# Input projection and gated linear attention of a hybrid layer put into one program of slots, with half of the projection's weights reloaded

## The reference

```python
x = layer_norm(x, ln_in_g, ln_in_b)
gq, gk, gv, gr, glow, sq, sk, sv, cb, cc, ch = split_cols(x @ w_in)      # 1024 -> 3088 columns
lg = jax.nn.log_sigmoid((glow @ w_gate_up + b_gate).astype(f32)) / GLA_TAU
# gla_chunk, by chunks of 64 tokens:
b = jnp.cumsum(lg, axis=2)
att = jnp.einsum('bhtk,bhsk,bhtsk->bhts', q, k, decay)                   # decay = exp(b_t - b_s), s <= t
o = (jnp.einsum('bhtk,bhkv->bhtv', q * jnp.exp(b), S)
     + jnp.einsum('bhts,bhsv->bhtv', att, v))
S_new = (jnp.exp(b_last[:, :, 0, :])[..., None] * S
         + jnp.einsum('bhsk,bhsv->bhkv', k * jnp.exp(b_last - b), v))
# then
go = go * lax.rsqrt(jnp.mean(go * go, axis=-1, keepdims=True) + LN_EPS) * gla_norm_g * jax.nn.silu(gr)
cy, conv_state = short_conv(cc * ch, conv_prev, conv_w)                  # causal, 3 taps
co = cb * cy
```

## Time and profile before

| | |
|---|---|
| median of three runs (3108.27 to 3112.32) | 3112.1 us |
| the profiled execution, its own time | 3112.73 us |
| its span, first to last instruction | 3110.9 us |
| mean granted clock of TensorE | 0.934 of full speed |
| PE busy | 2734.4 us, 88% |
| DVE busy | 1505.1 us, 48% |
| ACT busy | 1069.5 us, 34% |
| POOL busy | 329.9 us, 11% |
| HBM traffic | 168 GB/s over the span |

### The profile page before, as it was taken

One profiled execution on the slowest core, in us unless ns is written; L12 is line 12 of the kernel. 1 busy time (PEld: TensorE's weight loads), 2 busy tenths in 40 slices (PEclk: granted clock), 3 DMA queues, 4 the chain that ended last, 5 costly groups with the idle time before them and its releaser, 6 DMA issues. The chain is left out here.

```text
span 3110.9 us, 38667 instructions
## 1 busy us (share of the span) xinstructions
PE 2734.4 (88%) x13838; PEld 2268.3 (73%) x13838; DVE 1505.1 (48%) x2247; ACT 1069.5 (34%) x1783; POOL 329.9 (11%) x283
## 2 busy tenths in 40 slices
PE   5999999946662467999998999999999988999997
PEld 4787789835541356888877888877888766888885
DVE  5333342158883556665656544446644425522224
ACT  3323333223342424443443444443434321322221
POOL 1100010056600000000001100001100000000000
PEclk9999999966786588999999999999999989999998
DMA  5544454233315654575655766565766554544452
GB/s 185 169 160 153 160 180 126 85 121 88 89 45 187 191 191 140 169 249 179 216 193 191 229 218 209 191 206 183 234 190 227 170 171 144 190 157 158 154 168 98
DMA packets 362107, 526.11 MB, mean 169 GB/s; under 512 B 28832, under 2 KB 208208, under 8 KB 361920
## 3 DMA queue, kind: packets, MB, share of 16 engines
q1 hardware_dynamic: 337696, 480.23, 48.1%
q10 hardware_dynamic: 18832, 26.10, 2.3%
q0 software_dynamic: 5392, 17.31, 1.6%
HBM read 422.74 MB, written 100.80 MB: 168 GB/s over the span
## 5 line engine op out<-in xcount | busy, mean ns | idle before, releaser
L111 PE MATMUL p_ps_u<-p_xh,p_wh 128*128 128x512 f32 (+1 forms) x1280 | 453.1, 354 | 5.4 <-DVE p_xl L1626 5.4
L112 PE MATMUL p_ps_u<-p_xh,p_wl 128*128 128x512 f32 (+1 forms) x1280 | 451.5, 353 | 0.0
L113 PE MATMUL p_ps_u<-p_xl,p_wh 128*128 128x512 f32 (+1 forms) x1280 | 451.0, 352 | 0.0
L1575 DVE SCALAR_TENSOR_TENSOR p_res<-p_res,p_ps_d 128x512 f32<-128x512 f32 (+1 forms) x340 | 232.1, 685 | 451.4 <-PE p_ps_d L113 445.7
L111 PE MATMUL p_ps_d<-p_wh,p_hh 128*128 128x512 f32 (+1 forms) x1088 | 433.2, 398 | 16.9 <-DVE p_res L1575 14.8
L112 PE MATMUL p_ps_d<-p_wh,p_hl 128*128 128x512 f32 (+1 forms) x1088 | 428.6, 394 | 0.0
L113 PE MATMUL p_ps_d<-p_wl,p_hh 128*128 128x512 f32 (+1 forms) x1088 | 428.4, 394 | 0.0
L1484 ACT ACTIVATE p_wh<-p_wst 128x1024 fp32r<-128x1024 f32 x288 | 293.9, 1049 | 276.6 <-PE p_ps_d L113 225.0
L1633 DVE TENSOR_TENSOR p_r<-p_r 128x512 f32<-128x512 f32 (+1 forms) x160 | 95.8, 599 | 461.3 <-ACT p_hh L1514 461.3
L1507 ACT ACTIVATE p_r<-p_ps_u 128x512 f32<-128x512 f32 (+1 forms) x160 | 83.8, 524 | 579.5 <-PE p_ps_u L113 579.4
L111 PEld LDWEIGHTS p_ps_u<-p_xh,p_wh 128*128 128x128 f32 x1280 | 241.2, 188 | 35.5 <-DVE p_xl L1626 6.2
(11 more groups left out here) (155 smaller groups left out, 4473.0 us busy)
## 6 DMA issues: line engine op xcount, KB each, us to landing
p_wl<-wlo_scratch SPq DMA_DIRECT2D x216, 512.0 KB, 5.1
p_wst<-in_w_up SPq DMA_DIRECT2D x128, 512.0 KB, 6.0
p_wst<-in_w_down SPq DMA_DIRECT2D x128, 512.0 KB, 4.6
wlo_scratch<-p_wl SPq DMA_DIRECT2D x72, 512.0 KB, 3.6
p_wst<-in_w_in SPq DMA_DIRECT2D x128, 256.0 KB, 3.6
p_kk<-ks_scratch SPq DMA_DIRECT2D x84, 256.0 KB, 5.9
p_vv<-vs_scratch SPq DMA_DIRECT2D x84, 256.0 KB, 4.5
p_wst<-in_w_out SPq DMA_DIRECT2D x32, 512.0 KB, 6.0
```

What stands on the lines that cost most here:

```text
L111: pe.matmul(out, lhs_hi, rhs_hi, start=first, stop=False, skip_group_check=skip)
L112: pe.matmul(out, lhs_lo, rhs_hi, start=False, stop=False, skip_group_check=skip)
L113: return pe.matmul(out, lhs_hi, rhs_lo, start=False, stop=last, skip_group_check=skip)
L1575: dve.scalar_tensor_tensor(out=acc, in0=acc, scalar=scale, in1=ps_d[:c, d % DB, :], op0=ALU.mult, op1=ALU.add).then_inc(d_free, 1)
```

## The change

`phase_in` and `phase_gla` become one program, `phase_head`. Its dense steps are those of the projection: 17 F steps (one of them the 16 columns of the gate) and four pairs of 256 columns of the T kind, whose tiles are one step each. The weights go in units of 128 x 1024 numbers, 24 per group, through a ring of four (`WRING`), with two raw units (`WSTG`). In the first group DVE makes the low halves and SP stores them to `wlo_scratch`; from the second group on the low half of a unit is loaded from there, and ACT still makes the high half from the raw weights. `xh` and `xl` are single, and three PSUM banks (`DB`) are left for the projection. GLA is cut into groups of 256 tokens and small slots: 12 or 13 for the ahead of a group (`ahead_slots`), 10 for its two tiles (`tile_slots`); behind each F step and each second T tile `take_slot` puts one of each kind, where its inputs allow it. What is left at the end of the dense list follows without dense steps in between (`drained`). The convolution has 18 pieces of up to 256 tokens; its loads (`c_load`) and its store (`conv`) stand in the common list and are issued by SP, and one piece is placed at a dense step once its inputs are two dense steps old. POOL keeps its arithmetic.

```diff
+def phase_head(nc, a, x_tile, wlo_dram, xn_dram, zt_dram, gv_dram, mixt_dram, k_p, v_p, k_s, v_s, lasting):
...
+    WRING, WSTG, DB, OUTS, XS = 4, 2, 3, 4, 5
+    GN = 256
+    GG = [(t, GN) for t in range(0, SEQ, GN)] + [(SEQ, DEC)]
...
+        pairs = [C_GV, C_GV + 256, C_SK, C_SV]
...
+        def t_steps(g, p):
+            u = weights("T", pairs[p], 0)
+            weights("T", pairs[p], 1)
+            return [("T", g, p, ti, u) for ti in range(len(gtiles[g]))]
...
+            more = gtiles[g + 1] if g + 1 < len(GROUPS) else []
...
+                dense += one + two
+            dense += [("x_load", t[0]) for t in more]
+            for i in range(len(fs)):
+                dense.append(("F", g, i, None if fs[i][1] == RANK else weights("F", fs[i][0])))
...
+            dense += t_steps(g, 2)
+            for ti, step in enumerate(t_steps(g, 3)):
```

```diff
+        def ahead_slots(g):
+            slots = [[("load", g)]] if g % 2 == 0 else []
+            slots += [[("gate", g), ("gate_log", g)], [("gate_sum", g)], [("decay", g), ("level_arg", g, 0), ("silu_exp", g)],
+                      [("level_mul", g, 0), ("level_arg", g, 1)]]
+            for li in range(NL):
+                slot = [("level_product", g, li)]
+                if li + 1 < NL:
...
+                if li == 1:
...
+            return slots + [[("level_product", g, li), ("level_put", g, li)] for li in (NL, NL + 1)]
...
+        def tile_slots(g):
+            js = group_tiles[g]
+            slots = [[("v_in", j) for j in js] + [("k_turn", js[0])], [("kv", js[0])]]
...
+                slots.append([("intra", j), ("inter", cs[0]), ("state", cs[0])] + [("k_turn", x) for x in more])
...
+                    slots.append([("inter", cs[1]), ("state", cs[1]), ("squares", j)])
...
+                slots.append([("sums", j), ("root", j)] + [("kv", x) for x in more])
+                slots.append([("gated", j)])
+            return slots
+        aheads, bodies = [ahead_slots(g) for g in range(NG)], [tile_slots(g) for g in range(NG)]
+        ag = body = 0
+        dense_at, order, next_w, drained = {}, [], 0, False
+        conv, conv_put = [(x, t, cnt) for t, cnt in GG for x in range(2)], 0
```

```diff
+        def take_slot():
+            nonlocal ag, body
+            found, a_before = [], ag
+            if body < NG and ag > body:
+                found += bodies[body].pop(0)
+                if not bodies[body]:
+                    body += 1
+            if a_before < NG and a_before <= body + 1:
+                f = dense_at.get(("F", source(a_before), gla_f))
+                if f is not None and (drained or f + 2 <= len(dense_at)):
+                    found += aheads[a_before].pop(0)
+                    if not aheads[a_before]:
+                        ag += 1
+            order.extend(found)
+            return bool(found)
...
+        def split_weights(i):
+            nonlocal next_w
+            while next_w < len(wunits) and (next_w < WRING or unit_end[next_w - WRING] < i):
+                order.append(("w", next_w))
+                if next_w + WSTG < len(wunits):
+                    order.append(("w_load", next_w + WSTG))
+                next_w += 1
...
+                dense_at[step[:3] if step[0] == "F" else step[:4]] = len(dense_at)
+                if step[0] == "F" or step[3] % 2 == 1:
+                    take_slot()
+                ready = [dense_at.get(("F", min(t // 512, 3), conv_f), len(dense_at)) for x, t, cnt in conv]
+                if conv_put < len(conv) and ready[conv_put] + 2 <= len(dense_at):
+                    order += [("c_load", conv_put), ("conv", conv_put)]
+                    conv_put += 1
+        drained = True
+        while True:
+            took = take_slot()
+            if conv_put < len(conv):
...
+        def wait_halves(eng, u):
+            if u < KINDS:
+                eng.wait_ge(wlo_done, u + 1)
+            else:
+                eng.wait_ge(whi_done, u + 1)
+                eng.wait_ge(wl_in[u % WRING], 16 * ((u - KINDS) // WRING + 1))
```

```diff
+                    sp.dma_start(wlo_dram[u], wl[:, u % WRING, :].bitcast(F32)).then_inc(wl_stored[u % WRING], 16)
+                elif what == "w":
+                    u = at[0]
+                    if u < KINDS + WRING:
+                        sp.wait_ge(wl_stored[u % WRING], 16 * KINDS // WRING)
+                    sp.wait_ge(m_mm, unit_count[u - WRING])
+                    sp.dma_start(wl[:, u % WRING, :].bitcast(F32), wlo_dram[u % KINDS]).then_inc(wl_in[u % WRING], 16)
...
+                elif what == "c_load":
+                    k = at[0]
+                    x, t, cnt = conv[k]
+                    if x == 0:
+                        wait_stores(sp, results_of(min(t // 512, 3), conv_f))
+                    if k:
+                        sp.wait_ge(c_out, 16 * k)
+                    for n, z in enumerate((Z_CC, Z_CH, Z_CB)):
+                        sp.dma_start(cin[:, n, :cnt], zt_dram[z + P * x:z + P * x + P, t:t + cnt]).then_inc(c_in, 16)
...
+                elif what == "conv":
+                    k = at[0]
+                    x, t, cnt = conv[k]
+                    sp.wait_ge(c_y, 6 * (k + 1))
...
-        phase_in(nc, x_tile, a["ln_in_g"], a["ln_in_b"], a["w_in"][0], a["ident"], xn_dram, zt_dram, token_stores, lasting)
-        phase_gla(nc, a, zt_dram, gv_dram, mixt_dram, lasting)
+        phase_head(nc, a, x_tile, wlo_dram, xn_dram, zt_dram, gv_dram, mixt_dram, k_p, v_p, k_s, v_s, lasting)
```

More of the change, by code:

```diff
@@ L179, in phase_in @@
-        units = []
-        for g, (t0, cnt) in enumerate(GROUPS):
-            for c, (pieces, kind, where) in enumerate(chunks):
-                gc = g * NCH + c
-                width = sum(w for _, w in pieces)
-                if kind == "F":
-                    for m0 in range(0, width, P):
-                        mw = min(P, width - m0)
-                        for o, cc in moving(cnt):
-                            units.append(dict(g=g, gc=gc, kind="F", m0=m0, mw=mw, o=o, n=cc, t0=t0, row=where + m0))
-                else:
-                    for o, cc in subtiles(t0, cnt, P):
-                        units.append(dict(g=g, gc=gc, kind="T", o=o, n=cc, t0=t0, what=where))
@@ new lines, in phase_head @@
+        unit_end = {}
+        for i, step in enumerate(dense):
+            if step[0] == "T":
+                unit_end[step[4]] = unit_end[step[4] + 1] = i
+            elif step[0] == "F" and step[3] is not None:
+                unit_end[step[3]] = i
+        def split_weights(i):
[5 more added lines that the diff above has]
+                next_w += 1
@@ L607, in _ @@
             sp.wait_ge(st_out, 32)
+            sp.wait_ge(cs_out, 64)
+            sp.wait_ge(c_out, 16 * len(conv))
             for q in range(2):
-                sp.wait_ge(on_st[q], 16 * len([j for j in range(len(tiles)) if j % 2 == q]))
+                sp.wait_ge(on_st[q], 16 * len(range(q, len(tiles), 2)))
+            for q in range(XS):
+                sp.wait_ge(xn_out[q], 16 * len(range(q, len(TILES), XS)))
         @block.scalar
@@ L792, in _ @@
+                    last.then_inc(lev_put, 1)
+                elif what == "state":
                     c = at[0]
@@ L877, in _ @@
                     mm.then_inc(k_turned, 1)
-                elif step == "kv":
+                elif what == "kv":
                     j = at[0]
@@ L908, in _ @@
                         pe.wait_ge(intra_done, 1)
-                elif step == "inter":
+                elif what == "inter":
                     c = at[0]
```

1136 lines of the change are left out of this document (539 added, 597 removed).

## The result

The changed kernel takes 3156.95 us (median of four, 3154.69 to 3158.98) beside 3111.93 before: a ratio of 1.0147, interval 1.013 to 1.0165. The forecast was 3102. The profiled execution has a span of 3154.4, and its tail starts at 1000.08 instead of 959.72. So 40.4 of the 43.5 us lie in the head, and 3.1 in the tail, which isn't edited.

A forecast was written before the change was run, and what follows sets the result against it. Projection bound by PE, GLA by no engine but a chain of short steps. Head terms 38 + 599 + 118 + 15 + 66 + 10 + 76 + 27 = 949 against 959.7, −10.7, hence 3102 us; range 3020 to 3165.

The forecast's parts named there:

- its own sign: Whole head: prediction wrong if PE has no pause over 8 us before the drained end, or head ends outside 900 to 1000.
- products and turns: Projection on PE: same products in new order, T kind at 256 columns costing 0.12 each, +7, hence 599 us.
- small products: Attention products in 83 slots between dense steps: 106 us of products plus 12 of drain at switches, 118 us.
- late operands of slots: Slots beside dense steps: group loads and v stand behind weight loads on SP, 15 us (0 to 30).
- v behind the last conv pieces, 27 us: Drained end: v's loads stand on SP behind the last conv store, so PE waits 27 us (10 to 35).
- Lead-in, 38 us: Kernel start: 29 to the first product, 3 for slow start, 6 for three handovers; 38 us (35 to 45).
- Half rate after the stalls, 10 us: PE products after each of seven stalls run at half rate, 1.5 us lost each, 10 us.
- The conv on SP's queue, 66 us: Dense groups: weights wait on SP behind conv pieces; PE loses 20 us in each of three groups, 6 in the last.
- The drained end, 76 us: After the dense list: 31 slots left with nothing beside them, 76 us to the next program.
- Hidden conv waits: Rival on SP's queue: conv waits don't hold PE; 3010 us (2995 to 3045), chance 0.14.
- Slot chains late: Rival at the 83 slots: DVE and ACT results come 0.6 us late each, adding 50; 3156 (3130 to 3200), chance 0.25.
- Reloaded low halves late: Rival on weight reloads: low halves land too late, 1 us for each of 72 units, 3174 us; chance 0.03.

## Why the prediction was wrong

The mechanism was the one that the forecast named, and it stands in the trace at the places named. What failed is the size of terms: v was 22 us too small, the products 15, lead-in and late operands 6 each, while the stalls were 4 too large; and the gain forecast, 10.7, was smaller than either of the first two. The head ended at 1000.08, at the edge of the 900 to 1000 that the forecast gave as its own sign. The head, term by term, forecast and measured, the half rate and the handovers counted with the products they stand in:

| term | forecast | measured |
|---|---|---|
| lead-in with three handovers | 35 | 41.2 |
| products and turns | 624 | 638.9 |
| small products beside them | 106 | 109.5 |
| late operands of slots | 15 | 20.7 |
| stalls behind the convolution | 66 | 62.1 |
| drained end | 76 | 79.4 |
| wait for v in it | 27 | 48.8 |
| to the tail's start | 949 | 1000.6 |

(The measured column is the sum of the distances of successive starts in PE's timeline by kind, with the idle before each counted by its releaser; 1000.08 is the row, 0.5 is rounding.)

*"v behind the last conv pieces, 27 us"* is the step that failed most, by 22 of 51 us. It took a 64-token piece for a short one and 3.6 for v's landing, from the median of before. The arithmetic of such a piece is short, as the row said; but its loads stood behind a store of state columns and its own load of columns took 8 to 9 us, so the pieces kept a cycle of 14 to 15, and v landed after 11. The run with these stores moved behind v puts 27 us on it, and leaves a wait for v of 24.3, near the 27 forecast. The column stores stood in the trace before too (POOL waited 14.7 us for them in two places), and I took their landing for a matter of the queue that waits for them.

*"Lead-in, 38 us"*: the first product came at 35.44 and not at 29.

*"Half rate after the stalls, 10 us"* and the products: 15 short. The half rate is 3 of them: a stall costs the products behind it 2.2 us on average (219 in place of 206 over six stalls), where it cost 1.5 with 512 columns. The other 12 lie in products and handovers and were not split further. The row price of 256 columns, 0.12, held to the digit in full-rate stretches, not the formula of the Trainium skill ("TensorE: Matmul & The Clock Gate", "Back-to-back issue gap"), which gives 0.109.

*"The conv on SP's queue, 66 us"* was right: 62.1, with two stalls per group (9.6 and 11.6, 7.9 and 9.8, 10.3 and 9.6) where 13 and 7 were worked out. The first of them came by the raw weights and ACT's list and not by a low half. *"The drained end, 76 us"* held (79.4) and *"small products"* too.

*The rivals.* "Hidden conv waits" would not have come out at 3010 but at 3034, by the version in which they are hidden; that is inside its range of 2995 to 3045 (its own terms, 66, 27 and most of 10, add up to some 100 and not to 93). "Slot chains late" named 3156, which is the time that was measured (its own sum, 3102 + 50, gives 3152), for a reason that did not apply: with the queue free, `qb`, `att` and `sq` cost under 6 us before the drained end. That it agrees is chance. "Reloaded low halves late" was given a chance of 0.03 as a loss; with the queue free the reload is a gain of 22.6, which the forecast had at nothing; behind the convolution on SP's queue, leaving it out won 5.5.

*The sentence of the Trainium skill* ("DMA: Bandwidth & Descriptors", "Issuing engines are not separate DMA queues") that issuing on several engines saves only the issue time leaves out the wait in front of an issue: with it the choice of queue moved this kernel from 3187 to 3034. Where SP's wait was mostly met, the trace comes near it: 3046 on SP beside 3034 on POOL. Its other half, that transfers of all queues run on the same 16 DMA engines, fits what the column stores show: POOL's queue instead of SP's changed nothing (3157.35 beside 3156.95), a later place did.

*The tail* grew by 3.1 us, from 2151.2 to 2154.3, which the forecast had at nothing. In the other versions, with the same tail, it took 2151.5 to 2157.4, so this is within what differs from one version to the next, and its cause stays open.

## What to carry to other kernels

A wait on a queue that issues transfers for several engines costs what stands behind it: list, for each wait on it, what stands behind and when that is wanted, and put the wait on the engine that has nothing behind it, or far enough down the list that it is already met. When a stage is put beside another, what remains at its end is priced by the latencies of its chain, and a wait there is not hidden by anything; the last, small pieces need their own sum. A gain forecast that is smaller than the error of its largest term says nothing of the sign.

## What the runs showed of the hardware

- Stores of two columns of state (256 numbers of 4 bytes) on POOL's queue delayed the transfers that SP issued behind them by some 7 us, as they did from SP's own: v landed after 10.5 us against 3.1, 64-token loads after 9.1 against 1.8. The stores of `go` and of the attention's state behind one landed after 6.1 to 6.6 us against 1.9.
- Behind an idle of 8 to 12 us PE's products of 256 columns stood 0.21 apart for the next 13 to 24 products (a granted clock of 0.50, 1.2 GHz, in the tile at 219), and 0.12 apart at 2.4 GHz; behind the idle of 2.9 us at 850.97 they stood 0.12 apart from the second on.
- DVE at half load was not free: 72 more operations of 1.2 us, with raw units held longer for them, cost 22.6 us.
